# The heads' gates by ScalarE's Sigmoid instead of Exp, addition and reciprocal

## The reference

```
u = rms_norm(x, norm_gain)
proj = u @ w_in                     # q, k, v, z of 8 + 8 heads of 128, indexer, 2 gates
o_sb = stick_breaking(q_sb, k_sb, v_sb)
y_sb = (o_sb * silu(z_sb)) @ w_branch_sb
o_sa = indexed_sparse_attention(q_sa, k_sa, v_sa, q_ix, k_ix, w_ix)
y_sa = (o_sa * silu(z_sa)) @ w_branch_sa
mixed = sigmoid(g_sb) * y_sb + sigmoid(g_sa) * y_sa
out = rms_norm(x + mixed @ w_out, final_norm_gain)
```

## Time and profile before

| what | value |
|---|---|
| time, median of 3 runs | 1655.31 us (1655.13 to 1656.64) |
| span of the profiled execution | 1654.6 us |
| PE busy | 1619.6 us |
| VectorE busy | 761.2 us |
| ScalarE busy | 576.4 us |
| granted clock of TensorE, mean | 0.996 |
| table loads on ScalarE | 4 |

### The profile page before, as it was taken

The page is one execution under the profiler, slowest core; times in us unless marked ns, Lnnn a source line. Parts: engine busy times, 40 slices in busy tenths (PEclk is TensorE's granted clock), DMA queues, the critical chain, the costliest instruction groups (busy, mean ns, idle before and its releaser), DMA issues.

```text
span 1654.6 us, 20303 instructions
## 1 busy us (share of the span) xinstructions
PE 1619.6 (98%) x7444; PEld 1356.0 (82%) x7444; DVE 761.2 (46%) x1096; ACT 576.4 (35%) x905; POOL 28.1 (2%) x40
## 2 busy tenths in 40 slices
PE   3999999999999999999999999999999999999997
PEld 3888888888888888888888888888888888888886
DVE  7334477722224444454344555454455544434333
ACT  4333334222224443354433333333233433313222
POOL 3000000000000000000000000000000000000000
PEclk9999999999999999999999999999999999999999
DMA  4332222333332322323222423332332422253222
GB/s 168 102 102 76 90 86 81 102 102 101 95 96 89 95 80 78 96 83 99 93 83 83 127 82 95 95 95 82 96 95 89 173 100 102 89 200 124 95 103 115
DMA packets 81003, 166.94 MB, mean 101 GB/s; under 512 B 6976, under 2 KB 6976, under 8 KB 79680
## 3 DMA queue, kind: packets, MB, share of 16 engines
q1 hardware_dynamic: 77920, 152.72, 28.8%
q0 software_dynamic: 3040, 13.63, 2.1%
HBM read 157.94 MB, written 8.39 MB: 101 GB/s over the span
## 4 chain that ended last, share of the span: by engine, by line
PE 97%; DVE 2%; DMA 1%; ACT 0%; SPq 0%; issue 0%
PE proj L1023 28%; PE proj L1024 28%; PE proj L1025 28%; PE attn L1024 3%; PE attn L1025 3%; PE attn L1023 3%; PE attn L1159 1%; DMA xs<-in_x 1%; PE attn L1188 1%; PE attn L1120 1%; PE attn L1119 1%; DVE tmp L672 0%; DVE tmp L670 0%; DVE u_lo L690 0%; PE proj L1074 0%; PE attn L1161 0%
## 5 line engine op out<-in xcount | busy, mean ns | idle before, releaser
L1023 PE MATMUL proj<-u_hi,w_hi 128*128 128x512 f32 x1536 | 600.0, 391 | 0.0
L1024 PE MATMUL proj<-u_lo,w_hi 128*128 128x512 f32 x1536 | 598.1, 389 | 0.0
L1025 PE MATMUL proj<-u_hi,w_lo 128*128 128x512 f32 x1536 | 597.9, 389 | 0.0
L647 DVE TENSOR_TENSOR w_lo<-stage,w_hi 128x1024 fp32r<-128x1024 f32 x267 | 325.8, 1223 | 537.7 <-ACT w_hi L358 535.1
L358 ACT ACTIVATE w_hi<-stage 128x1024 fp32r<-128x1024 f32 x267 | 281.8, 1060 | 509.2 <-PE proj L1025 373.9
L1025 PEld LDWEIGHTS proj<-u_hi,w_lo 128*128 128x128 f32 x1536 | 288.3, 188 | 60.4
L1023 PEld LDWEIGHTS proj<-u_hi,w_hi 128*128 128x128 f32 x1536 | 288.5, 188 | 58.5
L1024 PEld LDWEIGHTS proj<-u_lo,w_hi 128*128 128x128 f32 x1536 | 288.5, 188 | 58.2
L374 ACT ACTIVATE area<-proj 128x512 f32 (+1 forms) x80 | 47.9, 599 | 171.3 <-PE proj L1025 171.2
L1023 PE MATMUL proj<-w_hi,u_hi 128*128 128x512 f32 x256 | 99.9, 390 | 0.0
L1025 PE MATMUL proj<-w_hi,u_lo 128*128 128x512 f32 x256 | 99.6, 389 | 0.0
(11 more groups left out here) (168 smaller groups left out, 1436.2 us busy)
## 6 DMA issues: line engine op xcount, KB each, us to landing
stage<-in_w_in SPq DMA_DIRECT2D x208, 512.0 KB, 3.6
stage<-in_w_out SPq DMA_DIRECT2D x32, 512.0 KB, 3.5
stage<-in_w_branch_sb SPq DMA_DIRECT2D x16, 512.0 KB, 3.5
stage<-in_w_branch_sa SPq DMA_DIRECT2D x16, 512.0 KB, 4.0
xs<-in_x SPq DMA_DIRECT2D x4, 1024.0 KB, 10.1
o_scratch<-og POOLq DMA_DIRECT2D x16, 256.0 KB, 2.3
hres<-in_x POOLq DMA_DIRECT2D x1, 4096.0 KB, 13.7
o_in<-o_scratch POOLq DMA_DIRECT2D x3, 1024.0 KB, 6.1
```

Of the source, the lines that this page charges most:

```text
L647: V.tensor_tensor(w_lo[:, s % RING, :, :], stage[:, s % 2, :, :], w_hi[:, s % RING, :, :].bitcast(F), ALU.subtract).then_inc(strip_lo, 1)
L1023: nc.tensor.matmul(out_, a_hi, b_hi, start=start, stop=False, skip_group_check=free)
L1024: nc.tensor.matmul(out_, a_hi, b_lo, start=False, stop=False, skip_group_check=free)
L1025: return nc.tensor.matmul(out_, a_lo, b_hi, start=False, stop=stop, skip_group_check=free)
```

## The change

ScalarE writes `sigmoid(z)` in place of `exp(-z)`. VectorE's addition and reciprocal go, only the multiplication by z stays. The semaphore `gate_exp` becomes `gate_sig`, and `silu_step` counts one step per head in place of three.

```diff
-            def gate_exp_z(hh, z_slot):
+            def gate_sigmoid_z(hh, z_slot):
                 act.wait_ge(og_free, hh + 1)
                 apart()
-                A(og[:, :], area[:, ds(z_slot, 1), :], ACT.Exp, scale=-1.0).then_inc(gate_exp, 1)
+                A(og[:, :], area[:, ds(z_slot, 1), :], ACT.Sigmoid).then_inc(gate_sig, 1)
...
-                    act.wait_ge(silu_step, n * 3 + 3)
+                    act.wait_ge(silu_step, n + 1)
...
             def silu(hh, z_slot):
-                dve.wait_ge(gate_exp, hh + 1)
-                V.tensor_scalar(og[:, :], og[:, :], 1.0, None, ALU.add).then_inc(silu_step, 1)
-                dve.wait_ge(silu_step, hh * 3 + 1)
-                V.reciprocal(og[:, :], og[:, :]).then_inc(silu_step, 1)
-                dve.wait_ge(silu_step, hh * 3 + 2)
+                dve.wait_ge(gate_sig, hh + 1)
                 V.tensor_tensor(og[:, :], og[:, :], area[:, ds(z_slot, 1), :], ALU.mult).then_inc(silu_step, 1)
...
             def gated(hh):
                 dve.wait_ge(av_done, hh + 1)
-                dve.wait_ge(silu_step, hh * 3 + 3)
+                dve.wait_ge(silu_step, hh + 1)
```

More of the change, by code:

```diff
@@ L202, in build @@
     w_full, w_low, av_done = sem("w_full"), sem("w_low"), sem("av_done")
-    gate_exp, silu_step, o_ready, o_stored = sem("gate_exp"), sem("silu_step"), sem("o_ready"), sem("o_stored")
+    gate_sig, silu_step, o_ready, o_stored = sem("gate_sig"), sem("silu_step"), sem("o_ready"), sem("o_stored")
     lg_ready, max_ready, p_exp, inv_ready, p_ready = sem("lg_ready"), sem("max_ready"), sem("p_exp"), sem("inv_ready"), sem("p_ready")
@@ L518, in sb_steps @@
                 return [stage_qk(n, n, n + HEADS), s1, s2, s3,
-                        lambda: gate_exp_z(n, n + 3 * HEADS), s5, s6]
+                        lambda: gate_sigmoid_z(n, n + 3 * HEADS), s5, s6]
             for first, end in SA_LOOPS:
@@ L560, in sa_steps @@
                 return [stage_qk(hh, slot(0), slot(1)), lambda: v_high(slot(2)), s2, s3,
-                        lambda: gate_exp_z(hh, slot(3)), s5]
+                        lambda: gate_sigmoid_z(hh, slot(3)), s5]
             with act.Fori(0, 2) as a:
@@ L568, in _ @@
                     act.wait_ge(qk_lo, n * 2 + 2 * HEADS + 2)
-                    act.wait_ge(silu_step, n * 3 + 3 * HEADS + 3)
+                    act.wait_ge(silu_step, n + HEADS + 1)
                     evacuate(n + C_GATE, lambda e: area[:, ds(b * 8 + a + 2 * e, 1), :])
```

## The result

| | before | after |
|---|---|---|
| median | 1656.03 us (5 runs, 1655.13 to 1656.64) | 1662.33 us (5 runs, 1661.51 to 1662.72) |
| ratio | | 1.004 (95% interval 1.0029 to 1.005) |
| span of the profiled execution | 1654.6 us | 1660.8 us |
| VectorE busy | 761.2 us | 703.5 us |
| ScalarE busy | 576.4 us | 692.6 us |

The account below looks back on a forecast made before the run. PE, busy 98% of the span, was taken as the bound. Only loop-top loads cost: stalls 5.25 us plus slow starts 1.2, taken as 6.5, all else 0; 1655.3 + 6.5 = 1661.8 us, range 1658.5 to 1665.8.

Parts of the forecast that it names:

- Term 1: Table load at the loop's top in 12 heads delays kl past its cover, so PE stalls before the scores: 6.5 us.
- the slow start: After each of twelve stalls, the first score's weight load is partly exposed: 0.10 us per head, 1.2 us.
- Term 2: Seven loads inside Abs, Exp and Ln in each of 8 heads, hidden with 3.5 us of cover before the sums: 0.
- Term 3: Last loads of a head, ahead of the Sigmoid and the first weights: hidden, 1.9 us left at the weights, cost 0.
- Rival A: Each load holds ScalarE a second 1.28 us, giving waits at loop tops and sums: 66 us, 1721 us; chance 4%.
- Rival B: Loads all fall into ScalarE's idle time, including at the loop's top: no change, 1655.3 us; chance 8%.
- Rival C: VectorE's relief speeds PE's matmuls: 3.6 us back, 1651.7 us without the loop-top stalls, 1658 with them; chance 3%.

Follow-up runs that it names:

- experiment 2: Kernel before, gate untouched, with one table load at the top of the loop for heads 0 to 3 and 8 to 15: 1662.34 us, ratio 1.0037.
- experiment 3: Kernel before with seven table loads inside Abs, Exp and Ln of each of heads 0 to 7, none at a loop's top: 1655.90 us, ratio 1.0.
- experiment 1: Changed kernel with the joint table of Exp and Ln asked for by name right behind each Sigmoid, two loads per head: 1655.41 us, ratio 0.9999.
- experiment 4: Changed kernel, all 95 loads kept, with the q and k steps ahead of the strip 2 split at a head's top: 1655.95 us, ratio 0.9999.
- experiment 5: Kernel before without VectorE's addition and reciprocal, no added table load, gates left wrong: 1655.35 us, ratio 0.9999.

## Why the prediction was right

**Which places wait.** As forecast: the first scores of heads 0 to 3 and 8 to 15, twelve waits for `kl`, none in heads 4 to 7, none at the sums, none for a `w_lo`. Experiments 2 and 3 show that this is cause and not company. The sums of heads 4 to 7 follow each other every 50.59 us in both kernels, as forecast; ScalarE is busy for 116 us more and VectorE for 58 us less, where 117 and 60 were forecast.

**Term 1** was 6.5 us. The spacing of the first scores gives it back part by part. The one of head 15 starts at 1260.37 against 1254.28, 6.09 us later, and the changed execution had come to the heads 0.25 us earlier (the matmul at 509.55 against 509.80), so the heads cost 6.34 us. The stalls are 0.33 to 0.65 us and sum to 5.04 us, against 5.25; the slow start is 12 x 0.11 = 1.3 us, against 1.2, for which I had chosen between 0 and 0.22 us per head. The two small errors partly cancel, and that the slow start was hit so closely is in part luck. The load's delay in head 0 came out at the 1.42 us of the forecast. The 0.5 us by which the median lies above 1661.8 is not in the change: the forecast starts from 1655.3 us, and the runs of before beside the changed kernel have 1656.03.

**Term 2** was 0, with at least 3.5 us of cover left. In head 0 of the changed kernel the last `sp_low` ends at 529.76 and PE comes to the sums at 534.02:

```profile
529.01 0.75 DVE L829 TENSOR_TENSOR x_lo<-full,x_hi 128x256 fp32r<-128x256 f32 x2
```

```profile
534.02 0.39 PE L1155 MATMUL attn<-x_lo,neg_tri 128*128 128x512 f32 x1
```

That is 4.3 us of cover; the bound was kept, with 0.8 us to spare. Each load costs 1.28 us in the chain, not 1.30: from the end of an Exp to the start of its Ln 1.31 us pass with a load between them and 0.03 us without. Seven loads and PE's own 0.3 us make 9.3 us, and the last `sp_low` ends 8.7 us later than before. That idle moments of ScalarE, which the bound left out, absorb the difference is my inference. **Term 3**: the last load of a head ends at 534.58 and the weights begin at 537.37, 2.8 us of cover instead of the 1.9 of my bound:

```profile
533.30 1.28 ACT L492 ACT_TABLE_LOAD   x1
537.37 0.60 ACT L492 ACTIVATE full<-attn 128x512 f32<-128x512 f32 x1 [2.78 <-PE attn L1157]
```

**Rival A**, a switch that costs more than its record, falls: the next instruction starts 0.01 us after the load at 505.30, the 56 loads of experiment 3 are free, and the load lies on the line of the Copies. The seven loads inside Abs, Exp and Ln of the changed kernel, which switch tables by the compiled order, delay `sp_low` by no more than their records. The prediction had less behind it here than it says: of the four loads in the trace before only two have a neighbour within 0.02 us on both sides, 3.66 us pass behind the first load of the run and 7.51 behind the last, and the earlier trace rows show no neighbour at all. The Trainium skill, ScalarE: Activation LUTs, section What ACT_TABLE_LOAD costs, has 1283 ns for the load, which all 95 rows confirm, and adds a drain of about 1380 ns for every switch. This trace does not show one: behind 85 of the 95 loads the next instruction starts within 0.02 us, and ahead of none but the first is ScalarE idle for more than 0.24 us. The measurement decides, and here a load delays what follows by 1.42 us at most. The rule in section Table sets: the hidden batching unit of the same page of the Trainium skill, to batch activations by set, points the right way here, but what it is worth is decided by 12 of the 95 loads.

**Rival B**, loads in idle time, is not what the changed kernel does, but it is what experiments 1 and 4 make of it: 1655.41 and 1655.95 us, against the 1655.3 us that it was priced at. **Rival C** falls with experiment 5: 1655.35 us where it asked for 1651.7.

**What the prediction had not seen.** Its price for a wait of PE was linear: idle time and a slow start. That is true of the waits that the change makes, 0.3 to 0.7 us long, and of those of about 1 us with two Copies at the top and with five in the chain. It is not true of those of 2 us. So the 66 us that I gave for rival A, with idle times of several microseconds at the sums, would probably have been too low; no run makes waits of that length in the heads.

## What to carry to other kernels

A function that needs another table costs as many loads as the compiled order of ScalarE shows, not as many as the source suggests; where a loop begins with one table and ends with another, name the joint table at its end. What a load costs is read at its place: its 1.28 us and the lost overlap against the time by which the result is ready before the bounding engine asks. Here 83 loads were free and 12 cost 0.53 us each; a thin cover of one microsecond at the turn of a loop is where to look first.

## What the runs showed of the hardware

The clock of TensorE fell to 0.50 behind idle times of about 2 us in 12 of 20 cases (6 of 12 and 6 of 8 in the runs with three Copies at the top and with six in the chain), each fall costing 1.6 us more, but one, which lasted twice as long, 3.2 us. Behind the waits in the heads of other profiles, with 1.0 us or less in the list (20 in the run with five Copies, 12 each in the run with two Copies and in the changed kernel), it did not fall once. The same idle time of 1.97 us was followed by either clock, so its length alone does not decide; what else does, these runs leave open.

A table load is recorded with 1283 ns in every row, whether it brings in another table or the same one again. Between two instructions that would otherwise overlap it delays the second by 1.42 us, and in the chain of Abs, Exp and Ln by 1.28 us.
